# A retention head's two gates as seven block products, with weight sums added by DMA and operand sums kept in DRAM

## What is computed

```python
p_l = h_l @ w_in
q_l, k_l, v_l = _split_heads(p_l, bn, L)
...
of_l, _ = _retention_scan(q_l, k_l, v_l, log_gamma[0], s_f)
ob_l, _ = _retention_scan(flip(q_l), flip(k_l), flip(v_l), log_gamma[1], s_b)
gf_l, gb_l = _gates(p_l, bn, L)
...
y = _headnorm(o_f) * jax.nn.silu(g_f.astype(jnp.float32)) + _headnorm(o_b) * jax.nn.silu(g_b.astype(jnp.float32))
```

## Time and profile before

| | us |
|---|---|
| median of 3 runs (1958.47 to 1960.4) | 1959.24 |
| the profiled execution, its own time | 1959.92 |
| its span in the trace | 1958.1 |
| TensorE busy | 1945.9 (99% of the span) |
| VectorE busy | 1312.5 (67%) |
| ScalarE busy | 642.7 (33%) |
| GpSimd busy | 385.9 (20%) |

### The profile page before, as it was taken

The page is one execution under the profiler, slowest core; times in us unless marked ns, Lnnn a source line. Parts: engine busy times, 40 slices in busy tenths (PEclk is TensorE's granted clock), DMA queues, the critical chain, the costliest instruction groups (busy, mean ns, idle before and its releaser), DMA issues.

```text
span 1958.1 us, 25025 instructions
## 1 busy us (share of the span) xinstructions
PE 1945.9 (99%) x9525; PEld 1668.2 (85%) x9525; DVE 1312.5 (67%) x1892; ACT 642.7 (33%) x894; POOL 385.9 (20%) x360
## 2 busy tenths in 40 slices
PE   9999999999999999999999999999999999999998
PEld 6889889889889988899888888888888888888887
DVE  4756678688778776777865553644554477777778
ACT  3423222234323322232533223313323344344443
POOL 0300311322222222112350110020020026100004
PEclk9999999999999999999999999999999999999999
DMA  9623334335898998898322132121222125976656
GB/s 338 249 65 76 108 123 130 94 118 151 203 249 209 217 230 221 238 231 206 114 70 65 54 102 65 54 92 54 75 65 81 58 83 173 241 217 188 181 142 149
DMA packets 110833, 282.95 MB, mean 144 GB/s; under 512 B 16256, under 2 KB 29184, under 8 KB 110592
## 3 DMA queue, kind: packets, MB, share of 16 engines
q1 hardware_dynamic: 84496, 219.34, 33.8%
q0 software_dynamic: 24400, 58.21, 17.0%
q10 hardware_dynamic: 1824, 3.85, 0.6%
HBM read 234.67 MB, written 2.12 MB: 121 GB/s over the span
## 4 chain that ended last, share of the span: by engine, by line
PE 92%; DVE 2%; POOL 2%; DMA 2%; issue 2%; ACT 1%; SPq 0%; POOLq 0%; DVEq 0%; ACTq 0%
PE bank L999 17%; PE bank L1001 17%; PE bank L1000 17%; PE bank L1038 7%; PE bank L1039 7%; PE bank L1037 7%; PE bank L1400 3%; PE bank L1402 3%; PE bank L1403 3%; PE bank L1604 2%; PE bank L1602 2%; PE bank L1605 2%; PE bank L1307 1%; PE bank L1356 1%; PE bank L1219 1%
## 5 line engine op out<-in xcount | busy, mean ns | idle before, releaser
L2099 DVE TENSOR_TENSOR w_lo<-raw,w_hi 128x1024 fp32r<-128x1024 f32 x132 | 171.4, 1298 | 244.5 <-ACT w_hi L1628 244.4
L1628 ACT ACTIVATE w_hi<-raw 128x1024 fp32r<-128x1024 f32 x132 | 139.4, 1056 | 371.4 <-PE bank L1039 198.6
L1037 PE MATMUL bank<-w_hi,hT_hi 128*128 128x512 f32 x592 | 230.8, 390 | 0.0
L1038 PE MATMUL bank<-w_lo,hT_hi 128*128 128x512 f32 x592 | 230.5, 389 | 0.0
L1039 PE MATMUL bank<-w_hi,hT_lo 128*128 128x512 f32 x592 | 230.5, 389 | 0.0
L999 PE MATMUL bank<-w_hi,act_hi 128*128 128x512 f32 x504 | 198.4, 394 | 0.0
L1001 PE MATMUL bank<-w_hi,act_lo 128*128 128x512 f32 x504 | 196.6, 390 | 0.0
L1000 PE MATMUL bank<-w_lo,act_hi 128*128 128x512 f32 x504 | 196.5, 390 | 0.0
L999 PE MATMUL bank<-hT_hi,w_hi 128*128 128x384 f32 (+2 forms) x544 | 192.4, 354 | 0.0
L1001 PE MATMUL bank<-hT_hi,w_lo 128*128 128x384 f32 (+2 forms) x544 | 191.0, 351 | 0.0
L1000 PE MATMUL bank<-hT_lo,w_hi 128*128 128x384 f32 (+2 forms) x544 | 191.0, 351 | 0.0
(11 more groups left out here) (390 smaller groups left out, 4337.0 us busy)
## 6 DMA issues: line engine op xcount, KB each, us to landing
raw<-w_units_d SPq DMA_DIRECT2D x242, 512.0 KB, 3.8
mod<-mod_units_d SPq DMA_DIRECT2D x64, 384.0 KB, 4.4
wsum<-w_units_d SPq DMA_DIRECT2D x45, 512.0 KB, 4.5
wsum<-w_units_d POOLq DMA_DIRECT2D x26, 512.0 KB, 7.7
wsum<-wsum POOLq DMA_DIRECT2D x19, 512.0 KB, 6.7
bv<-mod_units_d SPq DMA_DIRECT2D x16, 512.0 KB, 3.6
mod<-mod_units_d SPq DMA_DIRECT2D x14, 512.0 KB, 7.9
res_lat<-rbuf POOLq DMA_DIRECT2D x28, 256.0 KB, 5.1
```

The costliest lines, as they stand in the source:

```text
L1037: nc.tensor.matmul(bank[t][:, :], hT_hi[:, kc, tt], hi[:, c], start=kc == 0, stop=False)
L1038: nc.tensor.matmul(bank[t][:, :], hT_hi[:, kc, tt], lo[:, c], start=False, stop=False)
L1628: nc.scalar.activation(halves_of(phase, k, i)[0], raw[:, s, :], ACT.Copy).then_inc(hi_done, 1)
L2099: tt(lo, raw[:, s, :], f32(hi), ALU.subtract).then_inc(lo_done, 1)
```

## The change

Write the inputs of a head's gates as blocks A11, A12, A21, A22 (first or second 256 tokens by first or second 512 features) and the weights as B11, B21 (gate gb, first and second features) and B12, B22 (gate gf). The eight block products of before become seven: A11 by B11 (product 1), A12 by B21 (2), S4 by B22 (3), A22 by B12+B11+B22+B21 (4), S1 by B12+B11 (5), S2 by B12+B11+B22 (6) and S3 by B12+B22 (7), with S1 = A21-A22, S2 = S1-A11, S3 = A11-A21 and S4 = S2+A12 (tiles `s_gs`, `s_y`, and `s_q` for S3 and S4 in turn). A product is 24 matmuls of 512 columns in two banks. Four products (numbers 1, 6, 5, 3) stand between the scores and `of`, three (7, 2, 4) between `of` and `ob`:

```diff
+GATES = [(1, 0, True), (6, 2, True), (5, 4, True), (3, 6, True), (7, 6, True), (2, 0, False), (4, 6, False)]
+GATES_1 = 4
+def _gates(products):
+    out = []
+    for q, b, _ in products:
+        out += [(f"gu{q}", None, None)] + [(f"g{q}.{t}", b + t, "A" if q in (1, 2) else "D") for t in range(2)]
+    return out
...
+_HEAD += _gates(GATES[:GATES_1]) + [(f"of{t}", 2 + t, "D") for t in range(LAT)] + _gates(GATES[GATES_1:])
+_HEAD += [("ob3", 3, "D"), ("ob2", 2, "D"), ("ob1", 1, "D"), ("y3", 7, "D"), ("ob0", 0, "D")]
```

**Weights.** A head's gates had 8 unit loads. Now they have 6 plain loads, 8 loads of a base (B12) and 14 adding DMAs of GpSimd into the raw slot, in chains of 1, 2 or 3 adds. On the SP queue, with n the number of a split in the head (`GATE` is 8, `OUT` 22):

```diff
+                def plain(k, n, slot):
+                    sp.wait_ge(lo_done, split + n + 1)
+                    load(at + k, slot)
...
+                def base(k, n, slot):
+                    sp.wait_ge(lo_done, split + n + 1)
+                    sp.dma_start(raw[:, slot, :], w_units[at + k]).then_inc(t_base0[slot], 16)
...
+                def sum_out(x, tile):
+                    sp.wait_ge(s_lo0, 4 + SUMS1_AT[x])
+                    sp.dma_start(sums_d[x], tile[:, :, :].bitcast(F32)).then_inc(s_out, 16)
...
+                def sum_in(x, tile):
+                    sp.dma_start(tile[:, :, :].bitcast(F32), sums_d[x]).then_inc(s_in[x], 16)
...
+                for n in range(RAW):
+                    plain(4 + n, n, n)
+                if h:
+                    sp.wait_ge(pe_step, step_of(*head_at(h - 1), "y0"))
+                    sum_in(S2, s_y)
+                    sum_in(S1, s_gs)
+                for n in range(2):
+                    plain(GATE_UNITS["B11"][n], 4 + n, n)
+                base(GATE_UNITS["B12"][0], 6, 2)
+                if not h:
+                    sum_out(S1, s_gs)
+                base(GATE_UNITS["B12"][1], 7, 3)
+                if not h:
+                    sum_out(S3, s_pa[S3])
+                    sum_out(S2, s_y)
+                    sum_out(S4, s_pa[S4])
+                for n in range(2):
+                    base(GATE_UNITS["B12"][n], GATE + n, n)
+                sp.wait_ge(s_out, 64)
+                sp.wait_ge(pe_step, step_of(phase, i, f"s{TILES0 - 1}"))
+                sum_in(S4, s_q)
+                for n in range(2):
+                    plain(GATE_UNITS["B22"][n], GATE + 2 + n, 2 + n)
+                for n in range(2):
+                    base(GATE_UNITS["B12"][n], GATE + 4 + n, n)
+                for n in range(2):
+                    base(GATE_UNITS["B12"][n], GATE + 6 + n, 2 + n)
+                for n in range(2):
+                    plain(GATE_UNITS["B21"][n], GATE + 8 + n, n)
+                sp.wait_ge(pe_step, step_of(phase, i, "g3.1"))
+                sum_in(S3, s_q)
+                for n in range(RAW):
+                    plain(16 + n, GATE + 10 + n, n)
+                for n in range(RAW):
+                    plain(20 + n, OUT + n, n)
+            for h in range(HEADS):
+                head_loads(h)
```

and on GpSimd's queue:

```diff
+            def gate_sum(h, slot, blocks, bases, parts=0, only=None):
+                at = BASE["heads"]["units"] + 20 * h
+                for n, block in enumerate(blocks):
+                    if only is not None and n not in only:
+                        continue
+                    for j in range(2):
+                        if n:
+                            pool.wait_ge(t_sum0[slot + j], 16 * (SUMS0 + SUMS_HEAD[slot + j] * h + parts + n))
+                        else:
+                            pool.wait_ge(t_base0[slot + j], 16 * (BASES0[slot + j] + 2 * h + bases))
+                        nc.gpsimd.dma_start(raw[:, slot + j, :], w_units[at + GATE_UNITS[block][j]], accum_op=ALU.add)\
+                            .then_inc(t_sum0[slot + j], 16)
+            def head_sums(h):
+                gate_sum(h, 2, ["B11", "B22"], 1)
+                gate_sum(h, 0, ["B11"], 1)
+                gate_sum(h, 0, ["B22"], 2)
+                gate_sum(h, 2, ["B11", "B22", "B21"], 2, 2, (0, 1))
+                for t in range(2):
+                    power("heads", h, t, t)
+                gate_sum(h, 2, ["B11", "B22", "B21"], 2, 2, (2,))
+                for t in range(2, LAT):
                     power("heads", h, t, t)
                 for n, t in enumerate(reversed(range(LAT))):
                     power("heads", h, LAT + n, 4 + t)
```

```diff
+            def gates(phase, h, n, products):
+                for q, b, opens in products:
+                    at = GATE + 2 * [x[0] for x in GATES].index(q)
+                    x_hi, x_lo = GATE_OPERANDS[q]
+                    if q in GATE_SUM:
+                        x = GATE_SUM[q]
+                        if x in (S1, S2) and n == 0:
+                            pe.wait_ge(s_lo0, 4 + SUMS1_AT[x])
+                        else:
+                            pe.wait_ge(s_in[x], 16 * (n if x in (S1, S2) else n + 1))
+                    for part in range(2):
+                        pe.wait_ge(lo_done, before("splits", phase, h) + at + part + 1)
+                        hi, lo = halves_of(phase, at + part, h)
+                        for t in range(2):
+                            if part == 0:
+                                free(phase, h, f"g{q}.{t}")
+                            out, tt = bank[b + t][:, :], slice(t * P, (t + 1) * P)
+                            for kk in range(2):
+                                kc, c = 2 * part + kk, slice(kk * 512, (kk + 1) * 512)
+                                nc.tensor.matmul(out, x_hi[:, kc, tt], hi[:, c], start=opens and kc == 0, stop=False,
+                                                 skip_group_check=True)
+                                nc.tensor.matmul(out, x_hi[:, kc, tt], lo[:, c], start=False, stop=False, skip_group_check=True)
+                                last = nc.tensor.matmul(out, x_lo[:, kc, tt], hi[:, c], start=False, stop=kc == KC // 2 - 1,
+                                                        skip_group_check=True)
+                            if part == 1 or t == 1:
+                                last.then_inc(pe_step, 1)
```

**Combining.** VectorE combines the products before ScalarE can apply Silu, now from and to `gs`; `common` adds product 6 to product 1, which ScalarE copied out, and so on, for two tiles each:

```diff
+                def common(j):
+                    ended(6, j)
+                    dve.wait_ge(act_drain, drained(phase, i, f"g1.{j}")[1])
+                    tt(rbuf[:, j, :], bank[2 + j][:, :], rbuf[:, j, :], ALU.add).then_inc(dve_drain, 1)
+                def less_common(j):
+                    ended(5, j)
+                    done(f"g6.{j}")
+                    tt(gy[:, j, :], bank[4 + j][:, :], rbuf[:, j, :], ALU.subtract).then_inc(dve_drain, 1)
+                def gate_c12(j):
+                    ended(3, j)
+                    done(f"g5.{j}")
+                    tt(gs[:, j, :], bank[6 + j][:, :], gy[:, j, :], ALU.add).then_inc(dve_drain, 1)
+                def gate_c22(j):
+                    ended(7, j)
+                    tt(gs[:, 2 + j, :], gy[:, j, :], bank[6 + j][:, :], ALU.subtract).then_inc(dve_drain, 1)
+                def gate_c21(j):
+                    ended(4, j)
+                    tt(gs[:, 2 + j, :], bank[6 + j][:, :], rbuf[:, j, :], ALU.add).then_inc(dve_drain, 1)
...
+                forward = [(LAT, 0, 256, 512), (LAT + 1, 0, 128, 512)] + [(kt, kt * P, 0, 512 - kt * P) for kt in range(LAT)]
+                decayed(0, 6, 4, forward, range(6), {1: (2,), 2: (3,), 3: (4,), 4: (5,)})
+                common(0)
+                common(1)
+                split_lo(phase, i, GATE + 6)
+                split_lo(phase, i, GATE + 7)
+                dve.wait_ge(res_added, before("add", phase, i))
+                less_common(0)
+                less_common(1)
+                split_lo(phase, i, GATE + 8)
+                split_lo(phase, i, GATE + 9)
+                if first:
+                    dve.wait_ge(s_out, 64)
+                gate_c12(0)
+                gate_c12(1)
+                split_lo(phase, i, GATE + 10)
+                of_statistics(0)
+                split_lo(phase, i, GATE + 11)
+                of_gated(0)
+                of_statistics(1)
+                of_gated(1)
+                of_statistics(2)
+                of_statistics(3)
+                backward = [(LAT, 0, 128, 512), (LAT + 1, 0, 0, 512)]
+                backward += [(kt, 0, 640 - kt * P, (kt + 1) * P) for kt in reversed(range(LAT))]
+                decayed(1, 12, 10, backward, range(3), {})
+                gate_c22(0)
+                gate_c22(1)
+                decayed(1, 12, 10, backward, range(3, 6),
+                        {3: (12, lambda: of_gated(2)), 4: (13, lambda: of_gated(3))})
+                gate_c21(0)
+                gate_c21(1)
```

**Operand sums.** The operand sums are formed once, in the first head, by VectorE (7 elementwise passes and 4 low parts) and ScalarE (4 high parts), written to DRAM (4 MB in all) and read back, 1 MB at a time, four times in each later head and twice in the first. VectorE in the first head:

```diff
+                if first:
+                    dve.wait_ge(stage_lo, before("stage", "heads"))
+                    dve.wait_ge(res_base, BASE_RES["ln0b"] + LAT)
+                    whole_operand(kcs(gx21[:, :]), first_k, g_second)
+                    whole_operand(kcs(gx22[:, :]), second, g_second)
+                    whole_operand(kcs(gx11[:, :]), first_k, g_first)
+                    dve.wait_ge(x_whole, 7)
+                    operand1_sum(gx22, gx21, gx22)
+                    operand1_sum(gx21, gx11, gx21)
...
```

(14 more changed lines are left out.)

271 lines of the change are left out of this document (184 added, 87 removed).

## The result

The changed kernel takes **1980.62 us** (median of 4 runs, 1978.72 to 1983.06) against 1959.03 for the kernel before on the same chip: a ratio of 1.0108, 95% interval 1.0095 to 1.0120, so 21.6 us slower. The forecast was 1957.7 with a range up to 1972: wrong, above the range.

What follows compares the result with a forecast made beforehand. TensorE, busy 1945.9 of 1958.1 us, was taken as the bound. -21.8 removed + 4 x 3.7 waits + 1.8 + 1.3 first head + 2.4 last head = -1.5 us, giving 1957.7, range 1944 to 1972.

Steps and rivals of the forecast that it cites:

- What is removed: Gates on TensorE: 24 fewer matmuls a head at 0.2267 us, 5.44 us a head, 21.8 us over four heads.
- Up to the forward result: First four gate products: splits and sums in time, costed at nothing, with cover of 1.5 to 3 us in each product.
- The add for product 7: Product 7's weight sum: base lands in 3.5 us, add in 7.3, split done at 1226.1, 9 us before needed.
- What is queued behind it: ScalarE and VectorE work behind product 7's splits makes product 4 late: waits of 2.9 and 0.8, 3.7 us a head.
- The three-add chain for product 4: Product 4's weight sum: three adds after its base end at 1243.5, in time with 3 us to spare.
- The floor: Product 4 with instant adds: VectorE's chain behind the forward result still loses at least 1.5 us a head.
- First head: VectorE passes ahead of value unit 6's split lose 1.8 us; 1.3 us more allowed for sums going out.
- Last head: Three splits between ob3 and ob2 on VectorE delay the transposes of y1: 2.4 us lost.
- The backward result: Product 4's combinings and two splits ahead of ob3's statistics: starts 2.5 us later but catches up by ob0, costed at nothing.
- quick adds: Rival, 25%: adds in the heads land quickly, the loss is the floor of 1.5 us a head, time 1947.6.
- Slow adds: Rival, 22%: paired adds in the heads land in 10.2 us, 7.2 us lost a head, time 1974.
- The queue held by the read: Among missed waits, 8%: SP's queue held by an operand read waiting for product 3; mostly slower, 1963 to 1975.

Runs made afterwards that it cites:

- run 15: Run 13 with VectorE splits moved in the first and last head and product 5's sum an adding DMA too, 8 adds a head: 1948.57 us, ratio 0.9939.
- run 1: Changed kernel with the read of S3 issued as soon as product 3 ended, ahead of product 2's loads: 1995.29 us, ratio 1.0179.
- run 4: Changed kernel without the operand reads for products 3 and 7, which use A22 instead; adds stay: 1980.68 us, ratio 1.0104.
- run 2: Changed kernel without product 7's adds, its weights B12 alone, 12 adds a head: 1974.64 us, ratio 1.0080.
- run 5: Changed kernel without product 4's six adds, its weights B12 alone, 8 adds a head: 1975.28 us, ratio 1.0082.
- run 3: Changed kernel with all 14 adding DMAs a head left out, each product taking its base block alone: 1949.30 us, ratio 0.9946.
- run 6: Changed kernel with all 56 adds writing over the slot instead of adding, same transfers, queue and waits: 1964.95 us, ratio 1.0028.
- run 7: Changed kernel with sums made in place on what a slot holds, 8 loads and 10 adds a head: 1972.81 us, ratio 1.0068.
- run 10: Run 7 with VectorE's order changed, two forward gatings moved behind product 4's splits: 1962.49 us, ratio 1.0011.
- run 9: Changed kernel with VectorE's order alone changed, two forward gatings moved behind product 4's splits: 1976.62 us, ratio 1.0082.
- run 13: Run 12 with only product 5's sum left to GpSimd; products 6, 7 and 4 summed by in-place adding DMAs, 6 a head: 1950.09 us, ratio 0.9951.
- run 12: Changed kernel with products ordered 1, 5, 3, 6, 7, 2, 4 and weight sums on GpSimd except product 7's, 2 adding DMAs a head: 1965.73 us, ratio 1.0029.

## Why the prediction was wrong

- *What is removed*: right. 24 matmuls a head at 0.2267 us; without the adds the kernel took 1949.3, and in run 15 the gates take their bare 50.3 us in two heads.
- *Up to the forward result, costed at nothing*: right in heads 2 to 4 (21.76 us each), wrong in the first, 4.6 us late, where 1.3 was allowed for sums going out; the first head's product 4 is the latest of the four.
- ***The add for product 7***, **the first step that failed, in size.** Base landing 3.5 assumed, 6.1 and 4.8 measured; add 7.3 assumed, 8.1 and 9.5 measured in that head. The split ended at S+28.0 in place of S+24.7. I had said of the add that pairs and a lighter load work against each other, and took the middle; but the lighter load was read from the kernel before (0.22), and the change itself fills the DMA engines in just this stretch (0.93).
- ***What is queued behind it***, **the second, in kind.** The chain was the right one, but I costed every plain load in it at its landing in the kernel before. Product 2's second unit landed 7.7 us after its issue (the first 5.4) and held ScalarE 4.31 us, and S3's read, issued when product 7's slots were split, landed 11.5 us later. Step by step in the second head, VectorE's low part for product 7 ends 3.3 us later after S than forecast, that of product 2's second unit 6.8 us later, and product 4's 6.1 us later (S+53.9 for S+47.8). Of the 3.7 us a head, 6.8 to 13.6 were measured. The place that I named, product 4, is the one that sets the loss; the stop that one sees, 4.5 us a head at product 7 for S3's read, I had nowhere, and it lies in front of that later start without adding to it.
- *Missing altogether*: the granted clock. In the changed kernel it costs nearly nothing of its own, since product 4 waits for VectorE in any case. It does cost where the stop stands at product 4: 7.4 us in run 1 and 8.5 in run 4, by what product 4 takes there over the four heads (31.5 and 32.6 us, 24.1 in the changed kernel).
- *The three-add chain for product 4, in time*: ScalarE never waited for it in the head followed, but its third adds were issued at 1252.5 and 1254.3, S+41, behind two `rstd`, 6 us after the S+34.6 that I had, and its traffic delays the others (runs 2 and 5).
- *The floor*, 1.5 us a head: 1.2 in run 3. *First head*: the stop at unit 6 was 1.80 us for 1.8 predicted. *Last head*: 1.9 for 2.4. *The backward result at nothing*: right; from the gates' end to the next S the changed kernel takes 104.6 to 104.8 us, as before.
- *Rivals*: quick adds are refuted, since no add of 56 landed under 5.2 us, and their 1947.6 is 33 us under the measured time. The Trainium skill (DMA: Bandwidth & Descriptors, anatomy of one DMA on the gpsimd path) gives about 2.0 us plus bytes over 436 GB/s, which is an estimate of 3.2 us for 512 KB. This trace disagrees for its adds, and run 6 for plain writes on the same queue, which took 3.7 us at least and 4.7 in the median. Slow adds (22%, 1974) was nearest, with its mechanism half right: full DMA engines, but the plain loads and the read suffer with the adds. The queue held by the read (in the 8%) is what the longest waits of the changed kernel seem to show, and runs 1 and 4 refute it as the cause: without that stop the loss is as large or larger.

What the loss is made of, as far as runs show: 31.3 us hang on the adds (run 3); half is the adding as such (15.7 us, run 6); with fewer transfers (run 7), VectorE's order (10.3 us from run 7 to run 10, 4.0 from the changed kernel to run 9) and the products' order (12.4 from run 10 to run 13) nearly all comes back. These are not parts of a sum, since each edit counts only once the others let it. Open is how the 12.4 us divide: run 13 has another order of products, four fewer adding DMAs a head, product 5's sum and four combinations made by GpSimd, and an earlier read of S3. Run 15, with two of the adds put back, is no slower.

## What to carry to other kernels

A transfer's landing time belongs to the load on the DMA engines after the change, not before: add up what the change issues in the very stretch where it is needed, plain loads that stand beside it too. Sums that grow in the slot which already holds their first part need fewer transfers, and the order of products and of VectorE's work decides how long each add may take; with 7.4 us a landing the same idea goes from 1.1% slower to 0.6% faster. Don't take the longest wait for the cause: here the wait at product 7 lay in front of a start of product 4 that VectorE set. And price a stop of TensorE with its half clock only where nothing behind it waits anyway.

## What the runs showed of the hardware

- **An adding DMA costs more than a write of the same bytes.** 56 transfers of 512 KB: as adds, the software queue takes 25.0% of the 16 engines' span (494.9 us of 1979.5), as writes 21.3% (419.0 of 1967.0), without them 17.1% (333.2 of 1948.4, run 3). So by the packets' time an add takes 2.9 us of all 16 engines, (494.9 - 333.2) / 56, and a write 1.5, (419.0 - 333.2) / 56.
- **Half clock around a stop.** In the first head of the changed kernel the granted clock fell to 0.50 at 1086.0, 4.2 us into TensorE's stop of 5.12 us and 0.9 us before its end, and stayed there for 6.8 us, with matmuls 0.43 us apart in place of 0.227. In the third and fourth heads, with stops of 2.28 and 4.57 us, it fell 1.0 and 0.7 us behind the stop, for 3.4 us. In the second head of run 1 it fell 5.0 us into a stop of 10.11 us and stayed for 10.2 us. The same stop of 1.8 us at value unit 6 was not followed by it in the changed kernel and in runs 5, 6, 7, 9 and 12, and was in runs 2, 3, 4 and 13; the window with the stop in the changed kernel and in run 13:

```profile
1015.00:1025.00 10.00, 8.20 (x37) 6.45 (x36) 9.93 (x9) 4.81 (x5) 0.92 (x1) 1.00 0.51 164
```

```profile
1015.00:1025.00 10.00, 8.19 (x29) 6.25 (x28) 9.90 (x9) 4.13 (x4) 2.28 (x1) 0.83 0.42 157
```

  What decides it for so short a stop stays open.
- **GpSimd and VectorE get in each other's way.** GpSimd's two 128x1024 additions ran from 1210.32 to 1216.45, 3.1 us each; VectorE's low part of 1.23 us, begun in the first, took 2.82, and its next of 0.55 us took 2.74 and ended behind the second (run 12). The Trainium skill (SBUF — State Buffer, two separate sides) says that the ports which the two share are locked for a whole instruction and the other engine fully blocks. This trace agrees in the main: the two instructions of VectorE took 1.6 and 2.2 us more than elsewhere and ended 0.8 and 0.4 us behind GpSimd's first and second addition (the first one's end is an estimate, half of the 6.13 us row).
